# Feed-forward ends: first output products copied by ScalarE, last output weights in places of their own, four banks, and an embedding in three split products

## What is computed

```python
    h = h + rms_norm(mix @ w_out[i], g_mix_post[i])
    hn = rms_norm(h, g_ffn_pre[i])
    ff = (jax.nn.silu(hn @ w_ffn_gate[i]) * (hn @ w_ffn_up[i])) @ w_ffn_down[i]
    h = h + rms_norm(ff, g_ffn_post[i])
    e = rms_norm(p[i] @ w_ple_proj[i], g_ple[i])
    h = h + jax.nn.sigmoid(h @ w_ple_gate[i]) * e
```

## Time and profile before

| | |
|---|---|
| median of 3 runs | 2293.61 us (2293.08 to 2295.3) |
| profiled execution | 2300.83 us, span 2299.1 us |
| TensorE products | busy 2184.4 us, 95% of the span |
| VectorE / ScalarE / GpSimd | 57% / 35% / 45% |
| mean granted TensorE clock | 0.98 |

### The profile page before, as it was taken

One profiled execution on the slowest core, in us unless ns is written; L12 is line 12 of the kernel. 1 busy time (PEld: TensorE's weight loads), 2 busy tenths in 40 slices (PEclk: granted clock), 3 DMA queues, 4 the chain that ended last, 5 costly groups with the idle time before them and its releaser, 6 DMA issues.

```text
span 2299.1 us, 31376 instructions
## 1 busy us (share of the span) xinstructions
PE 2184.4 (95%) x12100; PEld 1870.5 (81%) x12100; DVE 1305.2 (57%) x1676; ACT 798.3 (35%) x1296; POOL 1031.3 (45%) x704
## 2 busy tenths in 40 slices
PE   7999989899998999989998999989999999999898
PEld 6999967799998888868896668768888888888576
DVE  2899988700039875740005645676666666666553
ACT  3454442112137752210115754322222222222353
POOL 2789941142236646023285531045555555555300
PEclk9999989999999999999999989999999999999899
DMA  4111122211100023211202013111111111112321
GB/s 132 56 37 37 58 70 91 96 53 52 38 19 1 1 74 129 83 56 55 111 1 79 1 56 113 61 37 37 55 53 47 55 55 55 55 52 77 117 74 46
DMA packets 110603, 136.60 MB, mean 59 GB/s; under 512 B 6977, under 2 KB 92609, under 8 KB 110367
## 3 DMA queue, kind: packets, MB, share of 16 engines
q1 hardware_dynamic: 110494, 135.08, 17.8%
HBM read 118.26 MB, written 16.81 MB: 59 GB/s over the span
## 4 chain that ended last, share of the span: by engine, by line
PE 77%; DVE 11%; POOL 4%; ACT 3%; issue 3%; DMA 2%; SPq 0%; POOLq 0%; DVEq 0%; ACTq 0%
PE PS L352 46%; PE PS L2318 17%; PE PS L1704 3%; PE PS L392 2%; POOL side_sum L532 2%; PE PS L1715 1%; PE PS L1744 1%; DVE att L1227 1%; PE PS L381 1%; PE PS L2613 1%; PE PS L1757 1%; DVE arg_b L1218 1%; DVE arg_a L1218 1%; DVE decay L1203 1%; DVE arg_b L1217 1%
## 5 line engine op out<-in xcount | busy, mean ns | idle before, releaser
L2492 DVE TENSOR_TENSOR ff_acc<-ff_acc,PS 128x512 f32<-128x512 f32 x336 | 227.5, 686 | 193.8 <-PE PS L352 192.5
L352 PE MATMUL PS<-xh,wh 128*128 128x352 f32 (+2 forms) x1024 | 321.8, 345 | 9.8 <-DVE xl L447 4.0
L352 PE MATMUL PS<-xl,wh 128*128 128x352 f32 (+2 forms) x1024 | 319.2, 342 | 0.0
L352 PE MATMUL PS<-xh,wl 128*128 128x352 f32 (+2 forms) x1024 | 318.2, 341 | 0.0
L2257 POOL TENSOR_TENSOR xl<-raw,xh 128x512 fp32r<-128x512 f32 x120 | 168.4, 1411 | 144.0 <-ACT xh L2369 144.0
L352 PE MATMUL PS<-wh,xh 128*128 128x256 f32 (+1 forms) x784 | 229.1, 317 | 4.0 <-DVE wl L343 2.8
L352 PE MATMUL PS<-wl,xh 128*128 128x256 f32 (+1 forms) x784 | 228.1, 316 | 0.0
L352 PE MATMUL PS<-wh,xl 128*128 128x256 f32 (+1 forms) x784 | 227.6, 315 | 0.0
L575 DVE SCALAR_TENSOR_TENSOR PS<-glu,conv_vec,PS 128x1040 f32<-128x1040 f32 x184 | 225.8, 1298 | 0.8
L352 PEld LDWEIGHTS PS<-xh,wh 128*128 128x128 f32 x1024 | 192.2, 191 | 22.0 <-issue 5.8
L352 PEld LDWEIGHTS PS<-xl,wh 128*128 128x128 f32 x1024 | 191.9, 190 | 11.5
(11 more groups left out here) (373 smaller groups left out, 4845.6 us busy)
## 6 DMA issues: line engine op xcount, KB each, us to landing
h_rows<-rows SPq DMA_DIRECT2D x24, 512.0 KB, 2.6
rows<-h_rows SPq DMA_DIRECT2D x24, 512.0 KB, 3.2
dn_raw<-in_w_ffn_down_dram SPq DMA_DIRECT2D x22, 512.0 KB, 3.6
raw<-in_gla_w_in_dram SPq DMA_DIRECT2D x10, 1024.0 KB, 5.1
raw<-in_w_ffn_gate_dram SPq DMA_DIRECT2D x20, 512.0 KB, 3.7
raw<-in_w_ffn_up_dram SPq DMA_DIRECT2D x20, 512.0 KB, 4.7
raw<-in_conv_w_in_dram SPq DMA_DIRECT2D x16, 512.0 KB, 4.8
raw<-in_w_in_dram SPq DMA_DIRECT2D x8, 1024.0 KB, 5.5
```

Of the source, the lines that this page charges most:

```text
L352: last = nc.tensor.matmul(out_of(c, cn), s, x[:, c0:c0 + cn], start=n == 0 and m == 0, stop=n == len(terms) - 1 and m == 2)
L2492: ins = nc.vector.tensor_tensor(x, x, PS[:, 6 + n % 2, :], ALU.add)
```

## The change

It touches the two ends of the feed-forward layer and the embedding.

- **Front, copies and banks.** The sixteen output products of pair 0 are copied to `ff_acc` by ScalarE (`keep_down`) instead of VectorE. They go round four banks (6, 7, 4, 5: `dn_bank`), and TensorE waits for the product four places earlier. Before `body(0)` it waits until all sixteen are copied.
- **Front, sum 4.** VectorE makes both parts of sum 4 ahead of `ff_low` of pair 1; ScalarE casts its high part between the twelfth and the thirteenth copy. Both are gone from `body(0)`.
- **Back, last output weights.** The last pair's high and low parts go into quarters of the activation buffer `xl7` that no product reads any more (`dn_weights`). ScalarE casts both halves straight after the silu of the last body and GpSimd subtracts both low halves in a row.
- **Back, banks.** The last pair's output products go round four banks too. TensorE first waits for all earlier adds and for the last use of bank 5.
- **Embedding.** `p` and `w_ple_proj` are split: `proj_h` by ScalarE and `proj_l` by GpSimd in the last body, `p_h` by ScalarE and `p_l` by VectorE (between its twelfth and thirteenth add of the last pair). `embed` becomes three split products, 12 instead of 8 recorded products a row tile.
- **Waits and places.** ScalarE no longer waits for GpSimd's last `ple_l` before the first `ff_norm`; TensorE still does before the gate products. The gain and row buffers of the final stage move from `A0` to `S0`, and their loads wait also for the last output products of the pair before and the last low part of the output weights.

The core of the diff:

```diff
+        def dn_bank(p, n):
+
+            return 4 + (n + 2) % 4 if isinstance(p, int) and p in (0, LAST) else 6 + n % 2
...
+            if isinstance(p, int) and p == LAST:
+                return xh7_last(half), xl7_last(half)
...
+            down_low(0, 0)
+            down_low(0, 1)
             first_operands(0)
...
             body(FPAIRS - 3, True)
+            pool.wait_ge(w_high, DN0 + 2 * FPAIRS + 1)
+            nc.gpsimd.tensor_tensor(proj_l[:], w_ple_proj[:], proj_h.bitcast(F32), ALU.subtract).then_inc(w_low, 1)
             for q in range(4):
                 ple_low(pool, nc.gpsimd, q).then_inc(matrix_lo, 1)
...
-                pe.wait_ge(dn_left, p * HALVES + (n + 1))
...
+                if dn_bank(p, 0) == dn_bank(p, 2):
+                    pe.wait_ge(dn_left, p * HALVES + (n + 1))
+                else:
+                    pe.wait_ge(dn_left, p * HALVES + max(n - 1, 1))
...
+            pe.wait_ge(combined, 1)
             for n in range(HALVES):
                 down(0, n)
+            pe.wait_ge(dn_left, HALVES + 2)
             pe.wait_ge(combined, 2)
...
             turn_p(pe)
+            pe.wait_ge(dn_left, LAST * HALVES + 2)
+            pe.wait_ge(combined, comb_at(FPAIRS - 3, 8))
             for n in range(HALVES):
-                down(FPAIRS - 1, n, True)
+                down(LAST, n)
...
                 if last:
+                    for half in range(2):
+                        down_high(LAST, half)
+                    act.wait_ge(raw_ready, pair_raw(FPAIRS - 2))
+                    nc.scalar.copy(proj_h, w_ple_proj[:]).then_inc(w_high, 1)
                     ple_high(act, 0)
...
             high(0, 0)
+            keep_down(0, 4)
             act.wait_ge(pool_own.sem, TERM0 + 2)
             high(0, 1)
-            act.wait_ge(dn_tile, NX)
+            keep_down(4, 8)
             down_high(1, 0)
+            keep_down(8, 12)
+            sum_high(4, 4)
+            keep_down(12, HALVES)
             ff_high(1, 0, A_, COMB0)
...
             product(1)
-            add_down(0, 0, HALVES)
+            dve.wait_ge(matrix_lo, 3)
+            sum_begin(4, f32(act_part(1, 0)), of_sum(2), ALU.subtract)
+            sum_rest(4, 4, f32(act_part(1, 0)), of_sum(2), ALU.subtract)
             ff_low(1, 0, A_)
             ff_low(1, 1, C_)
-            dve.wait_ge(matrix_lo, 3)
+            dve.wait_ge(dn_left, HALVES + 2)
             body(0)
...
-            add_down(FPAIRS - 1, 0, HALVES, True)
+            add_down(LAST, 0, 12)
+            dve.wait_ge(p_turned, 1)
+            dve.wait_ge(p_ready, 1)
+            nc.vector.tensor_tensor(p_l, banks(0, 4).rearrange("p (c n) -> p c n", n=HALF),
+                                    p_h[:].rearrange("p k (c n) -> p (k c) n", n=HALF).bitcast(F32), ALU.subtract).then_inc(p_ready, 1)
+            add_down(LAST, 12, HALVES)
...
-            sp.wait_ge(ff_tile, prod_done(last, 6))
+            sp.wait_ge(ff_tile, prod_done(last, 4))
+            sp.wait_ge(dn_tile, LAST * HALVES)
+            sp.wait_ge(w_low, DN0 + 2 * FPAIRS)
...
-                for k in range(2):
-                    for half in range(2):
-                        last = nc.tensor.matmul(PS[:, 6 + half, :], p_t[:, k, j * P:(j + 1) * P],
-                                                w_ple_proj[:, k, half * HALF:(half + 1) * HALF], start=k == 0, stop=k == 1)
+                rows = slice(j % 4 * P, j % 4 * P + P)
+                for half in range(2):
+                    last = products([(p_h[:, k, j * P:(j + 1) * P], p_l[:, 2 * k + j // 4, rows], proj_h[:, 2 * k + half, :], proj_l[:, 2 * k + half, :])
+                                     for k in range(2)], [(0, HALF)], lambda c, cn: PS[:, 6 + half, :])
...
-            nc.scalar.copy(p_t[:].rearrange("p k t -> p (k t)"), banks(0, 4)).then_inc(p_ready, 1)
-            act.wait_ge(matrix_lo, M9 + 4)
+            nc.scalar.copy(p_h[:].rearrange("p k t -> p (k t)"), banks(0, 4)).then_inc(p_ready, 1)
```

More of the change, by code:

```diff
@@ L208, in hybrid_block @@
         p_stage = at("p_stage", [P, KT, D], O0)
[L209 to L212, removed]
+        w_ple_proj, proj_l = at("w_ple_proj", [P, 4, HALF], W0), at("proj_l", [P, 4, HALF], W0, F32R)
+        p_h = at("p_h", [P, 2, SEQ], Z0 + 32768, F32R)
+        gain9 = [at(f"gain9_{s}", [P, D], S0 + s * 4096) for s in range(2)]
+        rows9 = [at(f"rows9_{s}", [P, D], S0 + 8192 + s * 4096) for s in range(2)]
         act9h = [at(f"act9h_{s}", [P, KT, P], A0 + 16384 + s * 8192, F32R) for s in range(2)]
@@ L2257, in low, with down_low @@
                 nc.gpsimd.tensor_tensor(lo, OP_AT[o], hi.bitcast(F32), ALU.subtract).then_inc(unit_ready, 1)
[L2259 to L2262, removed]
+            def down_low(p, half):
+                pool.wait_ge(w_high, p * 2 + (DN0 + half + 1))
+                hi, lo = dn_weights(p, half)
+                nc.gpsimd.tensor_tensor(lo, dn_raw[:, half * HALF:(half + 1) * HALF], hi.bitcast(F32), ALU.subtract).then_inc(w_low, 1)
             def first_operands(i):
@@ L2372, in down_high, with keep_down @@
                 act.wait_ge(raw_f_ready, p * 16 + (DN_RAW0 + 16))
-                cols = slice(half * HALF, (half + 1) * HALF)
-                nc.scalar.copy(dnh[:, cols], dn_raw[:, cols]).then_inc(w_high, 1)
+                nc.scalar.copy(dn_weights(p, half)[0], dn_raw[:, half * HALF:(half + 1) * HALF]).then_inc(w_high, 1)
+            def keep_down(first, last):
+                for n in range(first, last):
+                    j, half = dn_place(0, n)
+                    act.wait_ge(dn_tile, n + 1)
+                    nc.scalar.copy(ff_acc[:, j, half * HALF:(half + 1) * HALF], PS[:, dn_bank(0, n), :]).then_inc(dn_left, 1)
             def ff_high(p, half, src, need):
@@ L2385, in body @@
                 high(i, 2)
-                if isinstance(i, int) and i == 0:
-                    sum_high(4, 4)
                 act.wait_ge(pool_own.sem, i * 4 + (TERM0 + 4))
@@ L2410, in body @@
                 ff_high(i + 2, 1, C_, comb_at(i, 9))
-                down_high(i + 2, 1)
+                if not last:
+                    down_high(i + 2, 1)
             sum_high(1, 1)
@@ L2504, in body @@
             def body(i):
-                first = isinstance(i, int) and i == 0
                 p = i + 1
-                if first:
-                    sum_begin(4, f32(act_part(1, 0)), of_sum(2), ALU.subtract)
                 add_down(p, 0, 4)
```

60 lines of the change are left out of this document (32 added, 28 removed).

## The result

| | before | after |
|---|---|---|
| median of six runs each, us | 2293.87 | 2282.78 |
| profiled execution, us | 2300.83 | 2280.01 |
| its span, us | 2299.1 | 2278.3 |
| first output product of pair 0 to the end of the span | 790.38 | 776.71 |

The ratio is 0.9949, 95% interval 0.9932 to 0.9965: 11.1 us faster (8.0 to 15.6), where 19.1 was forecast. Nine later runs of the kernel after gave the same ratio, 0.9949 (0.9928 to 0.9969).

The account below looks back on a forecast made before the run. The prediction took TensorE, with 77% of the chain of waits and a full loop, as the bound, so gains lie at the two ends: -6.5 - 7.65 - 5.0 = -19.1, giving 2274.5 us on the median, range 2267 to 2283.

Parts of the forecast that it names:

- Front, -6.5: Start of the feed-forward: 2.1 late plus 1.9 slow stretch, less the 8.58 stop and 1.93 of slow products.
- the term of 2.1 us late: First output product of pair 1, waiting for ff_low, starts at 1528.1 instead of 1525.96 (1.1 to 4.4 late).
- Back, -7.65: Gate products of row tile 0 start at 2164.5 instead of 2172.15 (-9.15 to -5.7).
- What could hold that up: Back: GpSimd makes proj_l first, but ends ple_l at 2157.6, 7 us before the gate products ask.
- the last sixteen output products fit in 11 to 12 us: Sign that the back is right, for the output products before the embedding; they took 18.75 us before.
- The start at 2141.95 stays: The last sixteen output products begin when they did, since that hangs on ff_low of the first half.
- Gate products' clock: Tile 0's first sixteen gate products took 6.23 at clock 0.57, 2.6 over full; no gain counted (down to -2.6).
- Embeddings, -5.0: Seven later embeddings take 2.72 instead of 3.43 each as twelve split products, with weight loads fitting under them.
- (1): Four banks don't free the flow: the last sixteen products keep 0.91 each, costing 3.6 at the back; 2278, chance 0.14.
- (2): Runs outside the profile have less to lose: up to 7.2 of the gain is missing; to 2281.7, chance 0.10.
- (3): Weight loads stand in line with the embedding's products, 4.94 instead of 3.43 each: 2292, no change; chance 0.04.
- (4): Slower: the clock stays at 1.2 GHz through the tiles after the back's stops; four tiles give 2301; chance 0.05.

Follow-up runs that it names:

- GpSimd held: Kernel after, with GpSimd waiting for VectorE's last ffl before its five last subtractions; median 2286.78 us.
- in pieces: Kernel after, with each of GpSimd's five last subtractions made in four instructions of 128x512; median 2276.11 us, ratio 0.991.
- the front alone: Kernel before, plus only ScalarE's copies in four banks and sum 4 moved ahead of the loop; median 2289.23 us, ratio 0.9981.
- the early cast: Kernel after, with ScalarE's cast of sum 4 moved behind its first four copies, before its second high part; median 2279.15 us, ratio 0.9903.

## Why the prediction was right and where it failed

- **What bounds the kernel:** right; everything won or lost is at the two ends.
- **Front, -6.5, measured -5.0** to the loop's second pair of sums (66.53 to 61.50). The mechanism was the one described; the term of 2.1 us late measured 3.8 (21.04 from the first output product to the first of pair 1, 17.24 before). Of the 1.7, about 1.3 is the cast of sum 4, which ends 12.4 behind the first output product and not 11.1: ScalarE stood 2.05 for a GpSimd operation that VectorE's sum held. The slow stretch charged with 1.9 cost 1.7 here and 1.2 more in three other profiles of the same front, so -5.0 is the better of two outcomes.
- **Back, -7.65, measured -0.85** at the gate products. The step that failed is "What could hold that up": it dated GpSimd's earlier work well, but asked only whether it is done in time, not what it holds up while it runs. It now lies beside VectorE's last multiplications and ffl, which TensorE waits for. By its own sign (the last sixteen output products fit in 11 to 12 us) the back failed: they took 16.8, from 2132.59 on. "The start at 2141.95 stays" failed: 13.82 behind the three sums instead of 10.84 (10.99 with GpSimd held, 11.00 in pieces). The first add, which frees a bank, came 19.90 behind the three sums instead of 12.88 (12.88 again with GpSimd held). The earlier trace rows had the warning, 2.29 against 3.23; it was used for sum 4 and as a bound for p_l, which has one input in PSUM and took 2.28, as forecast. With the cause taken away, the embedding starts at 24.90 (forecast 24.99), and in pieces the gate products at 32.77, 8.27 less than before.
- **Gate products' clock:** counted as nothing, they gained 2.5 (6.23 in the earlier trace rows to 3.73), by a clock that this code does not always get. That and not the planned steps made -0.85 into -3.4.
- **Embeddings, -5.0:** measured -5.06, tiles 14.50 apart instead of 15.22; the weight loads fit under the split products, twelve of each in 2.73 us from 2170.83 on. The Trainium skill, TensorE: Matmul & The Clock Gate, Part 3, has the sentence that the prediction weighed, that a weight load overlaps products in flight only where the row groups differ; for these loads of all rows it does not hold.
- **The rivals.** (1) falls: with four banks an output product follows every 0.68 where nothing holds VectorE (2145.30 to 2145.98 after), with two every 0.90. (2) gave 2281.7, near the result, but its mechanism is not what the record shows: 7.1 of the profiled difference lay ahead of the change, where ten profiled executions of the same code put the first output product anywhere from 1495.74 to 1508.72; the -13.7 behind it lies inside the interval of the medians; and the back's old waits are the same, 29.56 and 41.02 for 29.59 and 41.04, in a profiled execution that is 13.5 us shorter (the front alone). (3) falls with the tile period. (4) falls as put, since no tile after the first is slow, but the clock does move the back by 2.5 to 4.5. (Its 0.43 for a slow product is 0.44 by its own division, 3.97 / 9; nothing hangs on it.)
- **The sum:** -5.2 - 3.4 - 5.06 = -13.7 instead of -19.1 on the profile, -11.1 in the medians. Of the 5.4 that are missing, 1.3 lie at the front and 4.2 between the three sums and the first sigmoid. The range, to 2283, held 2282.78 only just, and for a reason not among the rivals, which is luck.

## What to carry to other kernels

When work is moved on GpSimd, list what VectorE does in the new place with two SBUF operands: each such instruction can wait for the whole GpSimd instruction under way, and the other way round. If it is on the path, cut GpSimd's work into small instructions: the wait was then at most about one piece, and the gate products came 7.4 us earlier here, while holding GpSimd back moved the meeting elsewhere and brought 2.4. A cast that another engine's chain hangs on belongs ahead of the copies that merely free banks, best into a wait that the engine has anyway.

## What was not expected of the hardware

- GpSimd in instructions of 128x512, 128x2048 and 128x4096 made a VectorE operation of 0.69 last up to 1.76, 5.05 and 6.36 us; sums with one PSUM input ran beside it at 0.68.
- Cutting cost GpSimd little by itself: proj_l took 5.52 in four pieces with one VectorE multiplication let in between them, 4.64 in one. But each VectorE operation let in delays GpSimd: the sixteen pieces of ple_l took 23.29, where the four whole ones had taken 18.22 in a row before, and ended only 0.6 ahead of the first gate product.
- After the same pauses the clock came back at full for the gate products in two profiles (3.89 us for sixteen) and stayed near half, 0.54, with the early cast, whose back is the same code (6.7 us).
